# One block instead of two at the start of an encoder kernel: the modulation vectors and the input projection share one memory plan, and the first tile is modulated and split in halves

## The chip, the cores and the metric

The kernel runs on one core of one Trainium2 chip. A core has five engines that run side by side and meet through semaphores: TensorE (PE, matrix products into PSUM), VectorE (DVE), ScalarE (ACT), GpSimd (POOL) and SyncE (SP), which here does nothing but issue DMA transfers. The metric is the device time of one execution in microseconds (us).

## The reference

Two groups of rows (a prompt of 256 and a sample of 2048 rows, 1024 wide) go through one encoder layer with shared weights. What the change touches is its beginning:

```
mod = einsum('bd,de->be', silu(c), w_ada) + b_ada      # 2 x 6144
sh1, sc1, g1, sh2, sc2, g2 = split(mod, 6)
h = layer_norm(x) * (1 + sc1) + sh1
proj = einsum('bsd,de->bse', h, w_in)                  # 1024 -> 2048: q, k, v, u
lam = exp(sum(lq1 * lk1)) - exp(sum(lq2 * lk2)) + lambda_init
```

After that come rotary embedding, differential attention on q, k and v, a 2-D Fourier mix of u, an output projection, and a SwiGLU feed-forward part; they make up most of the time and are the same instructions in both kernels.

## The kernel before

The 2304 rows are 18 tiles of 128 rows (`NT`); tile `t` of the projection takes `x[ORDER[t]]`. The projection of a tile is 4 chunks of 512 columns by 8 blocks `k` of 128 inputs. For precision each product is made of three: both operands are split into a rounded high part and the remainder, and PE does hi times hi, hi times lo and lo times hi (`products`, L554 to L556). So a tile costs 96 products of 128x128 by 512 columns.

**The weights.** `w_in` comes in 32 pieces of 128x512 (256 KB; `w_in_piece(n)`, pieces 8c to 8c+7 belong to chunk c). Each piece passes three stations: SP loads it into one of four slots of the tile `ahead` (`w_raw`, `pair`), ACT copies it rounded into `w_hi`, DVE writes the remainder into `w_lo` (`split_w`, L240 in the first block, L690 in the second). A slot is free again when its remainder is written, so the load of piece n waits for `w_lo_done` of n-3, that is for the remainder of piece n-4. The high parts and remainders of all 32 pieces stay in memory for the other 17 tiles; only tile 0 has to wait for them.

**Two blocks.** A block is one program per engine between two barriers. `modulation` is the first. PE multiplies silu(c) by the two parts SH1 and SC1 of `w_ada`: eight steps `i` of 128 rows, each a pair of 512 KB loads into a ring of three slots `wa`, with 8 passes of 128x512 on PE (L213). DVE adds the bias (`add_bias`, L262), PE turns the rows into columns (L232), and DVE takes them (`take_cols`, L267). In between, the first two tiles of x are normalised on DVE (`norm`, L246 to L252), and tile 0 is transposed on PE (L222), modulated on DVE (L290, eight instructions, one for each k), copied rounded on ACT (L195) and its remainder taken on POOL (L205). SP issues all loads in one order, with the first 20 pieces of `w_in` between those of `w_ada`; 16 of them are also split. The block ends with some small DVE instructions for bias and lambda (L296 to L307).

At its end all engines meet at the block's barrier (L118), the semaphores of its scope are cleared, and they meet again (`Scope.release`, L74). Then `project` begins: PE transposes tile 1 (L549) and multiplies tile 0; DVE splits pieces 16 to 19, modulates tile 1 (L624), and splits pieces 20 to 31 with the normalisation of tile 2 after piece 27. Behind that DVE rotates q and k of tile 0 (`rotate`, L640 to L642). Chunk 0 of tile 1 may overwrite its PSUM bank when the rotation of tile 0's chunk 0 has read it (`turned_done`).

`project` itself ends with a barrier, the release of its own scope `proj`, and the release of the outer scope `w_in` that held what the two blocks shared; each release is a clearing of semaphores and a barrier.

Of the kernel before, what the change touches and what calls it, by code (L numbers as in the profile page):

```python
# [111 lines left out]
def modulation(nc, keep, first, x, rope, cT, w_ada, b_ada, lam_in, w_in, w_hi, w_lo):  # L112
# [4 lines left out]

    with ExitStack() as ctx:  # L118
        s = Scope(nc, ctx, "mod")
        RING, NCH = 3, 4  # L120
        wa = s.sb("wa", [P, RING, 2, D])
        c_in = s.sb("c_in", [P, KD, 2])
        c_silu = first["c_silu"]
        rows = s.sb("rows", [2, 2 * D])
        b_rows = s.sb("b_rows", [4 * KD, P])
        lam_v = s.sb("lam_v", [1, 4, QK])
        lam_p = s.sb("lam_p", [1, 2, QK])
# [2717 lines left out]
```

## Time and profile before

| what | value |
|---|---|
| median of 3 runs | 3055.91 us (3055.81 to 3057.52) |
| profiled execution | 3050.71 us, span of its instructions 3048.9 us |
| PE, DVE, ACT, POOL busy | 95%, 70%, 42%, 46% of the span |
| mean granted TensorE clock | 0.982 of full speed |

The span is the time from the first to the last instruction of one profiled execution; what lies around it is 1.8 us. "Idle before" in a row is the time that the engine stood still ahead of that instruction, with what ended the wait. The first block and the first tile of the second lie in the first 82 us of the span; the projection ends at about 504 us.

### The profile page before, as it was taken

Reading aid. Unit: us, or ns where it says so; the run is one execution under the profiler, and the core shown is the slowest. Engines: PE = TensorE matmul, PEld = TensorE weight load, DVE = VectorE, ACT = ScalarE, POOL = GpSimd, SP = SyncE. Lnnn points to the kernel's source line nnn. Section 1 sums busy time; section 2 is a strip of 40 time slices with the busy share of each in tenths; the row PEclk is TensorE's granted clock in tenths of the full one; section 3 lists DMA queues with packets and bytes.
Section 4 is the critical chain, followed back from the end, with each engine's and each line's share of the span. In section 5 each row is a group of like instructions: output and inputs, shape, how many; then the busy total and the mean of one; then the engine's idle time right before and its main releaser. Section 6 shows DMA issues by size and latency. Waiting matters only on the chain.

```text
span 3048.9 us, 39408 instructions
## 1 busy us (share of the span) xinstructions
PE 2902.0 (95%) x14244; PEld 2437.1 (80%) x14244; DVE 2139.3 (70%) x3093; ACT 1276.7 (42%) x2286; POOL 1409.1 (46%) x1110
## 2 busy tenths in 40 slices
PE   7999998899999998999689999999999999999996
PEld 3888886666666656888679999989999989999995
DVE  5666654988888865566566666677778666777767
ACT  2111112777777764456543233343333333333334
POOL 0233321011111125568745455475677566666655
PEclk9999999999999998999899999999999999999998
DMA  7333346221312105466431221242322224323322
GB/s 246 125 124 126 126 142 168 51 70 56 82 56 70 50 28 200 130 211 206 158 128 56 83 70 57 96 169 70 125 91 96 90 92 148 107 95 104 109 68 94
DMA packets 194061, 333.02 MB, mean 109 GB/s; under 512 B 15366, under 2 KB 102599, under 8 KB 193866
## 3 DMA queue, kind: packets, MB, share of 16 engines
q1 hardware_dynamic: 193868, 330.49, 33.5%
q8 instruction: 115, 1.88, 0.3%
q14 instruction: 78, 0.64, 0.1%
HBM read 250.72 MB, written 79.71 MB: 108 GB/s over the span
## 4 chain that ended last, share of the span: by engine, by line
PE 51%; POOL 3%; DVE 3%; issue 1%; DVEq 1%; POOLq 1%; ACT 1%; DMA 1%; SPq 0%; ACTq 0%
PE tail_bank L2306 9%; PE tail_bank L2308 9%; PE tail_bank L2307 9%; PE tail_bank L2330 5%; PE tail_bank L2331 5%; PE tail_bank L2332 5%; POOL tail_rounded L2042 1%; PE tail_bank L2245 1%; PE tail_bank L2243 1%; PE tail_bank L2244 1%; POOL tail_rounded L2050 1%; PE tail_bank L2192 0%; PE tail_bank L2184 0%; PE tail_bank L2185 0%; POOL tail_rounded L2055 0%
## 5 line engine op out<-in xcount | busy, mean ns | idle before, releaser
L2042 POOL TENSOR_TENSOR tail_rounded<-tail_plain,tail_rounded 128x512 fp32r<-128x512 f32 x462 | 649.2, 1426 | 490.8 <-ACT tail_rounded L1827 490.5
L2306 PE MATMUL tail_bank<-tail_rounded 128*128 128x384 f32 x1848 | 622.0, 337 | 35.4 <-ACT tail_plain L1847 10.4
L2307 PE MATMUL tail_bank<-tail_rounded 128*128 128x384 f32 x1848 | 620.4, 336 | 0.0
L2308 PE MATMUL tail_bank<-tail_rounded 128*128 128x384 f32 x1848 | 620.3, 336 | 0.0
L2466 DVE TENSOR_TENSOR tail_plain<-tail_plain,tail_bank 128x384 f32<-128x384 f32 x462 | 247.9, 549 | 283.8 <-PE tail_bank L2308 211.3
L1827 ACT ACTIVATE tail_rounded<-tail_plain 128x512 fp32r<-128x512 f32 x462 | 271.5, 621 | 377.3 <-DVE tail_plain L2444 184.3
L2306 PEld LDWEIGHTS tail_bank<-tail_rounded 128*128 128x128 f32 x1848 | 349.1, 189 | 39.8 <-issue 34.4
L2307 PEld LDWEIGHTS tail_bank<-tail_rounded 128*128 128x128 f32 x1848 | 349.2, 189 | 1.3
L2308 PEld LDWEIGHTS tail_bank<-tail_rounded 128*128 128x128 f32 x1848 | 349.0, 189 | 0.0
L1165 DVE TENSOR_REDUCE att_peak<-att_sc 128x1 f32<-128x1024 f32 x256 | 312.8, 1222 | 45.3 <-PE att_sc L978 38.5
L2330 PE MATMUL tail_bank<-tail_rounded 128*128 128x512 f32 x792 | 309.5, 391 | 16.1 <-issue 7.1
L1070 ACT ACTIVATE att_e<-att_sc,att_peak 128x1024 f32<-128x1024 f32 x256 | 285.4, 1115 | 80.4 <-DVE att_peak L1173 80.2
L2332 PE MATMUL tail_bank<-tail_rounded 128*128 128x512 f32 x792 | 309.5, 391 | 0.0
L2331 PE MATMUL tail_bank<-tail_rounded 128*128 128x512 f32 x792 | 309.4, 391 | 0.0
L2566 DVE TENSOR_TENSOR tail_plain<-tail_plain,tail_bank 128x512 f32<-128x512 f32 x348 | 230.8, 684 | 103.3 <-PE tail_bank L2332 99.0
L977 PE MATMUL att_sc<-held_w_hi 128*128 128x512 f32 x512 | 277.5, 542 | 20.9 <-ACT att_e L1070 13.4
L1015 PE MATMUL att_o<-att_w,att_v_s 128*128 128x512 f32 x512 | 260.3, 594 | 0.2 <-ACT att_o_sum L1081 0.2
L554 PE MATMUL proj_acc<-held_w_hi,w_in_h_hi 128*128 128x512 f32 x576 | 229.8, 399 | 0.0
L556 PE MATMUL proj_acc<-held_w_hi,w_in_h_lo 128*128 128x512 f32 x576 | 227.9, 396 | 0.0
L555 PE MATMUL proj_acc<-w_in_w_lo,w_in_h_hi 128*128 128x512 f32 x576 | 226.2, 393 | 0.0
L978 PE MATMUL att_sc<-held_w_hi 128*128 128x512 f32 x512 | 203.7, 398 | 0.0
L2330 PEld LDWEIGHTS tail_bank<-tail_rounded 128*128 128x128 f32 x792 | 149.1, 188 | 49.3 <-issue 8.0
(286 smaller groups left out, 5144.0 us busy)
## 6 DMA issues: line engine op xcount, KB each, us to landing
tail_plain<-in_w_gu SPq DMA_DIRECT2D x132, 512.0 KB, 4.8
keep_ahead<-in_w_dn SPq DMA_DIRECT2D x66, 512.0 KB, 6.6
proj_ada<-in_w_ada SPq DMA_DIRECT2D x16, 1024.0 KB, 5.9
held_w_hi<-scr_qs_d SPq DMA_DIRECT2D x128, 128.0 KB, 2.8
scr_h_d<-tail_plain SPq DMA_DIRECT2D x63, 256.0 KB, 4.5
tail_plain<-scr_h_d SPq DMA_DIRECT2D x45, 256.0 KB, 4.3
w_in_x_in<-in_x SPq DMA_DIRECT2D x18, 512.0 KB, 6.4
scr_att_d<-held_w_hi SPq DMA_DIRECT2D x36, 256.0 KB, 2.9
```

Of the source, the lines that this page charges most:

```text
L977: nc.tensor.matmul(dst, queries_at(w_hi, N // 2, 0, mp)[:, tokens], keys, start=True, stop=False)
L1015: ins = nc.tensor.matmul(o[:], v_s[:, m // (ST // 4) % 2, chunk, :], w[:, m % 2, chunk, :], start=(chunk == 0), stop=(chunk == ST - 1))
L1070: m = nc.scalar.activation(e[:, h * HALF:(h + 1) * HALF], sc[:, x % 3, :], ACT.Exp, bias=bias[:, 0:1], scale=SC, accum_out=sums[:, N % 2, ...
L1165: nc.vector.reduce_max(peak[:, N % 2, mp, h:h + 1], sc[:, x % 3, :], AX_X)
L1827: nc.scalar.activation(w_hi[:, j, :], operand(F, j), ACT.Copy).then_inc(whi_done, 1)
L2042: nc.gpsimd.tensor_tensor(w_lo[:, j, :], operand(F, j), w_hi[:, j, :].bitcast(F32), ALU.subtract).then_inc(wlo_done, 1)
L2306: nc.tensor.matmul(dst, w_hi[:, j, cols], h_hi[j][:, k, :], start=(k == 0), stop=False)
L2307: nc.tensor.matmul(dst, w_hi[:, j, cols], h_lo[j][:, k, :], start=False, stop=False)
L2308: m = nc.tensor.matmul(dst, w_lo[:, j, cols], h_hi[j][:, k, :], start=False, stop=(k == 3))
L2330: nc.tensor.matmul(dst, a_hi[:, i, c, tokens], dn_hi[:, i, cols], start=(i == 0), stop=False)
L2331: nc.tensor.matmul(dst, a_hi[:, i, c, tokens], dn_lo[:, i, cols], start=False, stop=False)
L2332: m = nc.tensor.matmul(dst, a_lo[:, i, c, tokens], dn_hi[:, i, cols], start=False, stop=(i == 1))
```

## The change

The two functions become one, `project`, with one block and one scope. Tiles that `modulation` had for itself now lie in tiles that the projection uses later: the ring `wa` in `ada`, `turned` and `u`, the bias rows in `work` (which also holds `part_sum`, `mid` and `v_out`), the lambda inputs in `h_raw`; the products of silu(c) go to `acc`, the columns, the bias and lambda to `qk_tp`. Gone are the barrier and the release between the blocks, and the release of the outer scope. The order on the engines changes in these places:

- the eight modulation instructions of tile 0 signal after the fourth (`h_half`); ACT and POOL make high part and remainder in two halves, and PE starts on the first four blocks k when the first half is there (`hlo_half`);
- PE transposes tile 1 after chunk 0 of tile 0 instead of ahead of it;
- ACT splits 10 pieces ahead of tile 0's high part (12 before) and pieces 10 to 17 behind it; DVE splits pieces 10 to 17 (`SPLIT_AHEAD`) ahead of tile 1's modulation, where it was 10 to 19;
- DVE splits pieces 0 to 2 between the normalisations of tiles 0 and 1;
- SP loads all 32 pieces in one stream, and tile 2 of x after piece 24, where it was after piece 19; the first load of `ada` has a wait for `ada_w_used` more;
- the small DVE instructions for bias and lambda stand behind piece 31, ahead of the first rotation.

```diff
-def modulation(nc, keep, first, x, rope, cT, w_ada, b_ada, lam_in, w_in, w_hi, w_lo):
...
+def project(nc, keep, x, cT, w_ada, b_ada, lam_in, mod_rows, w_in, w_hi, rope, qs_d, ks_d, v_d, up_d, fold_d, b0_d, mid_d, q_landed, k_first):
...
+        wa = [tile[:].rearrange(form).rearrange("p (h c) -> p h c", h=2) for tile, form in (
+            (ada, "p k c -> p (k c)"), (turned, "p a b c -> p (a b c)"), (u, "p k c -> p (k c)"))]
+        RING = len(wa)
+        rows = work[0:2].rearrange("r k c -> r (k c)")
...
+        SPLIT_AHEAD = 18
...
                 if u:
                     sp.wait_ge(half_done, u)
+                else:
+                    sp.wait_ge(ada_w_used, KD)
...
+            for n in range(pieces, PIECES):
+                piece(n)
+                if n == 3 * KD:
+                    load_x(2)
             load_ada(0)
...
-            for n in range(AHEAD, AHEAD + 4):
+            act.wait_ge(c_landed, 16)
+            nc.scalar.activation(c_silu[:], c_in[:], ACT.Silu).then_inc(silu_done, 1)
+            for n in range(10):
+                split_w(n)
+            act.wait_ge(h_half, 1)
+            nc.scalar.activation(h_hi[:, 0, 0:KD // 2, :], h_raw[:, 0:KD // 2, :], ACT.Copy).then_inc(hhi_half, 1)
+            act.wait_ge(h_done, 1)
+            nc.scalar.activation(h_hi[:, 0, KD // 2:, :], h_raw[:, KD // 2:, :], ACT.Copy).then_inc(hhi_done, 1)
+            for n in range(10, SPLIT_AHEAD):
                 split_w(n)
...
+            pool.wait_ge(hhi_half, 1)
+            nc.gpsimd.tensor_tensor(h_lo[:, 0, 0:KD // 2, :], h_raw[:, 0:KD // 2, :], h_hi[:, 0, 0:KD // 2, :].bitcast(F32),
+                                    ALU.subtract).then_inc(hlo_half, 1)
+            pool.wait_ge(hhi_done, 1)
+            nc.gpsimd.tensor_tensor(h_lo[:, 0, KD // 2:, :], h_raw[:, KD // 2:, :], h_hi[:, 0, KD // 2:, :].bitcast(F32),
+                                    ALU.subtract).then_inc(hlo_done, 1)
...
+            pe.wait_ge(hlo_half, 1)
             for t in range(NT):
-                if t + 1 < NT:
+                if 0 < t < NT - 1:
                     transposes(t + 1)
-                pe.wait_ge(hlo_done, t + 1)
+                if t:
+                    pe.wait_ge(hlo_done, t + 1)
...
                         if t == 0:
                             pe.wait_ge(w_lo_done, KD * c + k + 1)
+                            if c == 0 and k == KD // 2:
+                                pe.wait_ge(hlo_done, 1)
                         m = products(c, k, t % 2)
                     m.then_inc(chunk_done[c], 1)
+                    if c == 0 and t == 0:
+                        transposes(1)
...
                 if t == 0:
-                    for n in range(AHEAD + 4, PIECES):
+                    for n in range(SPLIT_AHEAD, PIECES):
                         split_w(n)
                         if n == PIECES - 5:
                             norm(2)
+                    dve.wait_ge(bias_turned, 1)
+                    nc.vector.tensor_copy(bias[:], bias_tp)
...
-        with ExitStack() as ctx_w:
-            weights = Scope(nc, ctx_w, "w_in")
```

**PE, from the last step of the modulation to the first products.** Before, from the sixteen small transposes of the modulation rows on:

```order
L232 MATMUL mod_cols<-keep_ident,mod_rows 128x2 x16
L118 UNCONDITIONAL_BRANCH
L540 UNCONDITIONAL_BRANCH
L549 MATMUL w_in_tp<-keep_ident,w_in_x_in 128x128 x8
L554 MATMUL proj_acc<-held_w_hi,w_in_h_hi 128x512
L555 MATMUL proj_acc<-w_in_w_lo,w_in_h_hi 128x512
L556 MATMUL proj_acc<-held_w_hi,w_in_h_lo 128x512
```

Now, where the 24 products of chunk 0 stand between the first and the last of these rows (L440 to L442 are the products, L435 the transposes of tile 1):

```order
L482 MATMUL proj_qk_tp<-keep_ident,proj_work 128x2 x16
L440 MATMUL proj_acc<-held_w_hi,proj_h_hi 128x512
L441 MATMUL proj_acc<-proj_w_lo,proj_h_hi 128x512
L442 MATMUL proj_acc<-held_w_hi,proj_h_lo 128x512
...
L435 MATMUL proj_tp<-keep_ident,proj_x_in 128x128 x8
L440 MATMUL proj_acc<-held_w_hi,proj_h_hi 128x512
```

The end of the block is gone from between them, and the transposes of tile 1 stand behind 24 products.

**DVE, from the normalisation of tile 0 to the splitting of the late pieces.** Before:

```order
L252 TENSOR_SCALAR w_in_x_in<-w_in_x_in,w_in_mv 128x1024
L246 BN_STATS w_in_stats<-w_in_x_in 128x6 x2
...
L240 TENSOR_TENSOR w_in_w_lo<-keep_ahead,held_w_hi 128x512 x10
L262 TENSOR_TENSOR mod_rows<-mod_acc,mod_rows 2x512 x4
L267 TENSOR_SCALAR keep_mod<-mod_cols 128x16 x2
L290 TENSOR_SCALAR w_in_h_raw<-w_in_tp,keep_mod 128x128 x8
L240 TENSOR_TENSOR w_in_w_lo<-keep_ahead,held_w_hi 128x512 x6
...
L690 TENSOR_TENSOR w_in_w_lo<-keep_ahead,held_w_hi 128x512 x4
L624 TENSOR_SCALAR w_in_h_raw<-w_in_tp,keep_mod 128x128 x8
L690 TENSOR_TENSOR w_in_w_lo<-keep_ahead,held_w_hi 128x512 x8
```

Now (L605 is `split_w`, L537 the modulation of a tile, L659 the first of the small instructions):

```order
L528 TENSOR_SCALAR proj_x_in<-proj_x_in,proj_mv 128x1024
L605 TENSOR_TENSOR proj_w_lo<-keep_ahead,held_w_hi 128x512 x3
L522 BN_STATS proj_stats<-proj_x_in 128x6 x2
...
L605 TENSOR_TENSOR proj_w_lo<-keep_ahead,held_w_hi 128x512 x7
L615 TENSOR_TENSOR proj_work<-proj_acc,proj_work 2x512 x4
...
L605 TENSOR_TENSOR proj_w_lo<-keep_ahead,held_w_hi 128x512 x8
L537 TENSOR_SCALAR proj_h_raw<-proj_tp,keep_mod 128x128 x8
L605 TENSOR_TENSOR proj_w_lo<-keep_ahead,held_w_hi 128x512 x10
...
L605 TENSOR_TENSOR proj_w_lo<-keep_ahead,held_w_hi 128x512 x4
L659 COPY proj_bias<-proj_qk_tp 128x32
```

Between the modulation of tile 1 and the last piece there were 8 + 4 = 12 pieces, and there are now 10 + 4 = 14.

**SP, the second half of the stream of pieces.** Before:

```order
L160 DMA mod_wa<-in_w_ada 128x1024 x2
L151 DMA keep_ahead<-in_w_in 128x512 x11
L118 UNCONDITIONAL_BRANCH
L360 UNCONDITIONAL_BRANCH
L372 DMA w_in_x_in<-in_x 128x1024
L411 DMA keep_ahead<-in_w_in 128x512 x12
L368 DMA proj_ada<-in_w_ada 128x4x512
```

Now:

```order
L258 DMA proj_turned<-in_w_ada 128x1024 x2
L249 DMA keep_ahead<-in_w_in 128x512 x16
L210 DMA proj_x_in<-in_x 128x1024
L249 DMA keep_ahead<-in_w_in 128x512 x7
L206 DMA proj_ada<-in_w_ada 128x4x512
```

The load of tile 2 of x (512 KB) moved from ahead of piece 20 to behind piece 24.

## Rows read from the trace of the kernel before

**Rows 1.** The page, busy time of each engine over the whole span:

```profile
PE 2902.0 (95%) x14244; PEld 2437.1 (80%) x14244; DVE 2139.3 (70%) x3093; ACT 1276.7 (42%) x2286; POOL 1409.1 (46%) x1110
```

**Rows 2.** All waits of PE from 80 to 503 us: total, times, longest:

```profile
PE w_in_tp L573 <- DVE w_in_h_raw L624: 3.2, 3, 1.9
```

**Rows 3.** Timeline of PE: start, us, instructions, [idle before <-releaser]:

```profile
25.11 3.60 PE L213 MATMUL mod_acc<-mod_wa,w_in_c_silu 128*2 128x512 f32 x8 [1.86 <-DMA mod_wa<-in_w_ada]
...
30.72 3.60 PE L213 MATMUL mod_acc<-mod_wa,w_in_c_silu 128*2 128x512 f32 x8 [0.99 <-DMA mod_wa<-in_w_ada]
...
35.02 3.59 PE L213 MATMUL mod_acc<-mod_wa,w_in_c_silu 128*2 128x512 f32 x8 [0.30 <-DMA mod_wa<-in_w_ada]
38.93 3.59 PE L213 MATMUL mod_acc<-mod_wa,w_in_c_silu 128*2 128x512 f32 x8 [0.32 <-DMA mod_wa<-in_w_ada]
43.38 1.15 PE L232 MATMUL mod_cols<-keep_ident,mod_rows 2*128 2x2 f32 x16 [0.85 <-DVE mod_rows L262]
55.35 1.94 PE L549 MATMUL w_in_tp<-keep_ident,w_in_x_in 128*128 128x128 f32 x8 [10.83 <-PEq L74]
56.95 0.78 PE L554 MATMUL proj_acc<-held_w_hi,w_in_h_hi 128*128 128x512 f32 x1
...
81.27 0.47 PE L554 MATMUL proj_acc<-held_w_hi,w_in_h_hi 128*128 128x512 f32 x1
```

**Rows 4.** Timeline of DVE in the same stretch:

```profile
44.90 2.64 DVE L290 TENSOR_SCALAR w_in_h_raw<-w_in_tp,keep_mod 128x128 f32<-128x128 f32 x8
...
53.32 0.17 DVE L296 COPY w_in_bias<-mod_cols 128x32 f32<-128x32 f32 x1
...
58.52 2.64 DVE L624 TENSOR_SCALAR w_in_h_raw<-w_in_tp,keep_mod 128x128 f32<-128x128 f32 x8
62.81 4.29 DVE L690 TENSOR_TENSOR w_in_w_lo<-keep_ahead,held_w_hi 128x512 fp32r<-128x512 f32 x4 [1.65 <-ACT held_w_hi L464]
...
72.28 1.28 DVE L609 BATCH_NORM_STATS2 w_in_stats<-w_in_x_in 128x6 f32<-128x512 f32 x2
...
77.61 0.69 DVE L690 TENSOR_TENSOR w_in_w_lo<-keep_ahead,held_w_hi 128x512 fp32r<-128x512 f32 x1 [0.25 <-ACT held_w_hi L464]
78.23 0.68 DVE L640 TENSOR_TENSOR proj_turned<-proj_acc,w_in_rot 128x512 f32<-128x512 f32 x1
...
79.49 0.68 DVE L640 TENSOR_TENSOR proj_turned<-proj_acc,w_in_rot 128x512 f32<-128x512 f32 x1
```

**Rows 5.** Timelines of ACT and POOL, tile 0's high part and remainder:

```profile
47.57 1.06 ACT L195 ACTIVATE w_in_h_hi<-w_in_h_raw 128x1024 fp32r<-128x1024 f32 x1 [6.02 <-DVE w_in_h_raw L290]
48.70 2.34 POOL L205 TENSOR_TENSOR w_in_h_lo<-w_in_h_raw,w_in_h_hi 128x1024 fp32r<-128x1024 f32 x1 [26.76 <-ACT w_in_h_hi L195]
```

**Rows 6.** Timeline of SP: issue of pieces 3 and 4, pair 5 of `w_ada`, pieces 24 on:

```profile
18.65 5.12 SPq L151 DMA_DIRECT2D keep_ahead<-in_w_in  x2
23.82 0.98 SPq L160 DMA_DIRECT2D mod_wa<-in_w_ada  x2
...
65.33 7.39 SPq L411 DMA_DIRECT2D keep_ahead<-in_w_in  x8
```

**Rows 7.** Timeline of ACT: it waits for piece 24:

```profile
68.56 0.63 ACT L464 ACTIVATE held_w_hi<-keep_ahead 128x512 fp32r<-128x512 f32 x1 [4.22 <-DMA keep_ahead<-in_w_in]
```

**Rows 8.** The tile `ahead`, to 82 us: remainders of the second block (min/median/max ns), time to landing:

```profile
L690 DVE TENSOR_TENSOR w_in_w_lo<-keep_ahead,held_w_hi x16: 677/692/2487, 55.8 to 77.6; 128x512 fp32r<-128x512 f32 x16
...
DMA to landing us min/median/max: 2.8/4.3/7.8
```

**Rows 9.** Stretches: length, busy of PE, PEld, DVE, ACT, POOL, clock, DMA, GB/s:

```profile
46.00:46.50 0.50, 0.00 (x0) 0.00 (x0) 0.50 (x3) 0.00 (x0) 0.00 (x0) 0.93 0.00 0
60.00:60.50 0.50, 0.50 (x3) 0.37 (x2) 0.50 (x3) 0.00 (x0) 0.00 (x0) 0.92 0.82 287
527.00:528.00 1.00, 1.00 (x5) 0.62 (x4) 1.00 (x2) 0.61 (x2) 0.00 (x0) 0.86 1.07 199
```

**Rows 10.** The releases' line at the end of the projection: first and last start:

```profile
L74 POOLq EVENT_SEMAPHORE  x4: 17/17/17, 511.0 to 511.6; - x4
```

More of the change, by code:

```diff
@@ L109 @@
 LATER = (SH2 * D, SC2 * D, G1 * D, G2 * D)
-def modulation(nc, keep, first, x, rope, cT, w_ada, b_ada, lam_in, w_in, w_hi, w_lo):
+def project(nc, keep, x, cT, w_ada, b_ada, lam_in, mod_rows, w_in, w_hi, rope, qs_d, ks_d, v_d, up_d, fold_d, b0_d, mid_d, q_landed, k_first):
     with ExitStack() as ctx:
[L119 to L127, printed above, removed]
+        s = Scope(nc, ctx, "proj")
+        NCH = 4
+        w_lo = s.sb("w_lo", [P, KD, WIDTH], F32R)
+        x_in = s.sb("x_in", [P, 2, D])
+        h_raw = s.sb("h_raw", [P, KD, P])
+        h_hi, h_lo = s.sb("h_hi", [P, 2, KD, P], F32R), s.sb("h_lo", [P, 2, KD, P], F32R)
+        rot = s.sb("rot", [P, 2, 2, QK])
+        stats, mv = s.sb("stats", [P, 2, 2, 6]), s.sb("mv", [P, 2, 4])
+        pair = keep["ahead"]
+        turned = s.sb("turned", [P, 2, 2, 512])
+        u = s.sb("u", [P, 4, 512])
+        ada = s.sb("ada", [P, KD // 2, 512])
+        work = s.sb("work", [P, 4, 512])
+        part_sum, mid, v_out = work[:, 0:2, :], work[:, 2, :], work[:, 3, :]
+        qk_hi = s.sb("qk_hi", [P, 2, HEADS, P], F32R)
+        qk_lo = s.sb("qk_lo", [P, 2, HEADS, P], F32R)
+        gate_cols = s.sb("gate_cols", [P, 2, 2, KD])
+        gate_rows = s.sb("gate_rows", [4 * KD, P])
+        bias = s.sb("bias", [P, 4 * KD])
+        c_in, c_silu = s.sb("c_in", [P, KD, 2]), s.sb("c_silu", [P, KD, 2])
         lam_s = s.sb("lam_s", [1, 8])
@@ L310, in project @@
[L310 to L329 removed]
+        tp = s.ps("tp", [P, KD, P])
@@ L471, in _ @@
                 if t == 0:
-                    for n in range(AHEAD + 4, PIECES):
+                    for n in range(SPLIT_AHEAD, PIECES):
                         split_w(n)
@@ L625, in modulate @@
                                                   keep["mod"][:, k, g:g + 1], ALU.mult, ALU.add)
+                    if t == 0 and k == KD // 2 - 1:
+                        ins.then_inc(h_half, 1)
                 ins.then_inc(h_done, 1)
@@ L702, in _ @@
                 if t == 0:
-                    for n in range(AHEAD + 4, PIECES):
+                    for n in range(SPLIT_AHEAD, PIECES):
                         split_w(n)
@@ L2743, in layer @@
         }
-        ahead = s.sb("ahead", [P, 4, 512])
+        keep["ahead"] = ahead = s.sb("ahead", [P, 4, 512])
         ctx_h = ctx.enter_context(ExitStack())
```

323 lines of the change are left out of this document (119 added, 204 removed).

## The prediction

> **What bounds the kernel now.** I read the page first: PE is busy for 95% of the span, every other engine for 70% or less [rows 1]. So a change of 80 us at the start can only pay by what it lets PE do earlier, and only if PE is then never again waiting for something that did not move. The waits of PE come next. From 80 us to the end of the projection at about 504 us PE waits 3.2 us in all, in three places of 18 tiles [rows 2]: from tile 1 on the projection is PE after PE, and the attention and the rest have the same instructions as before. The number to follow is therefore one: when does chunk 0 of tile 1 start? It starts at 81.27 us [rows 3]. Whatever it gains or loses reaches the end of the kernel, with what the end of the block changes.
>
> The timeline of PE shows what stands ahead of it. The modulation's four last pairs of `w_ada` start at 25.11, 30.72, 35.02 and 38.93 us, each after a wait for DMA, 8 passes in 3.6 us each; the last small transposes start at 43.38; then PE stands still for 10.83 us until 55.35, and the first product comes at 56.95 [rows 3]. In the gap lie the modulation of tile 0 on DVE (44.90 to 47.54), its high part on ACT (47.57 to 48.63), its remainder on POOL (48.70 to 51.04), and then only pieces, the small instructions from 53.32 on, and the barrier [rows 4, 5]. From the first product to tile 1 it is 81.27 - 56.95 = 24.3 us without a wait. The time spent there is PE's own. But the pieces are close behind: the remainder of piece 31 is finished at 77.61 + 0.69 = 78.30 us [rows 4], only some 1.5 us before PE reads it. What is to be seen: PE can start tile 0 ten microseconds earlier, but can it also end ten microseconds earlier? The stream of pieces decides that.
>
> **Part 1, the modulation.** SP issues pieces 3 and 4 from 18.65 us on and is held for 5.12 us, since piece 4 waits for the remainder of piece 1, which DVE, busy with and waiting for the normalisation of tile 1, has only by 23.3; so pair 5 goes out at 23.82 [rows 6]. The change takes piece 0's split ahead of that normalisation. SP's wait is for the count of remainders, one for piece 4, and is then met at about 18.3. Pair 5 can go out when PE has used pair 2, at about 20. Between the starts of pairs 6 and 7 lie 3.91 us, and in them the queue moved two pieces and a pair (1.57 MB); between the starts of pairs 4 and 5 it moved as much in 5.61 us [rows 3]. The difference, 1.7 us, is the emptiness that the early issue fills. PE's own work then binds: pair 4 at 25.11, its passes and tile 0's transposes to 29.7, and three more pairs of 3.5 us, with 0.5 us of small work, to 40.8; before it was 38.93 + 3.5 = 42.4. I take **1.6 us earlier** for everything that follows; the bounds are 0 and 1.7.
>
> **Part 2, the start of tile 0.** Modulation starts at 44.90 - 1.6 = 43.3. Half of it is 1.32 us; the half high part is an ACT instruction of the size of a piece, 0.63 us [rows 7]; half of POOL's 2.34 us [rows 5] is 1.2; with a tenth for each hand-over PE starts at 46.8, against 56.95 before. The second half is ready at 48.1, ahead of PE's need.
> PE starts slowly: the granted clock fell at about 46.4, two microseconds after PE's last work, and rose at about 60.0, 4.7 us after it began again [rows 9]. With the gap of about 3.8 us that is left I expect the same: to 51.3 at 1.2 GHz, a product each 0.43 us, then one each 0.229 us. Chunk 0 ends at 54.4, the transposes of tile 1 at 55.2.
>
> **Part 3, the pieces.** Here each step waits for the one before. ACT no longer splits pieces 10 and 11 early, so DVE has them at 48.6 and 49.2; a remainder that meets POOL's instruction waits for its end. (That is how I read the longest remainder, 2487 ns where the median is 692 [rows 8]: it starts at 62.81 [rows 4] beside POOL's remainder of tile 1.) The Trainium skill, "SBUF — State Buffer", section "SBUF: two separate sides", says the same: GpSimd and a DVE instruction with two SBUF inputs take one pair of ports by an exclusive lock, held for the whole instruction. By that rule the modulation of tile 0, which reads PSUM, would not be held by POOL's first half.
> Pieces 14 to 17 follow their slots and are done at 53.2 to 55.1. DVE then modulates tile 1 (2.64 us, [rows 4]) from 55.3 to 58.0. ACT and POOL follow to 61.5, and POOL holds the remainder of piece 18 until 62.05; 19 to 21 follow by 63.9.
> Now the ring of four sets the pace. Piece 24 was issued at 65.33 and ACT had it at 68.56, 3.2 us later [rows 6, 7]; the median to landing is 4.3 us [rows 8]. With 0.65 us on ACT and 0.69 on DVE a slot turns round in 4.6 to 6.4 us, and a burst of four lands about 0.9 us apart. Piece 22 (slot of 18) is done at 66.7, 23 to 25 by 69.3, where the load of x for tile 2 lies in the queue ahead of 25; 26 at 71.5, 27 at 72.3. Then come the normalisation of tile 2 and pieces 28 to 31, which before took from 72.28 to 78.30, 6.0 us with 0.25 of waiting [rows 4]; without the wait it is 5.8, and piece 31 is done at about **78.0 us**, against 78.30. The same stretch before gives the same: from the end of tile 1's modulation (58.52 + 2.64) to piece 31 it was 17.1 us for 12 pieces [rows 4]; from 58.0 with 14 pieces, the two more at 1 to 1.5 us each, it is 77 to 78.
> PE, ready early, waits for pieces from 22 on and ends tile 0 at 78.7.
>
> **Part 4, the small instructions.** They took from 53.32 to about 54.4 [rows 4]: 1.05 us. Before they lay under a wait of PE; now they stand between piece 31 and the rotation that PE waits for. The rotation of one chunk takes 79.49 - 78.23 = 1.26 us [rows 4]. So chunk 0 of tile 1 starts at 78.0 + 1.05 + 1.3 = **80.4 us**, against 81.27: 0.9 us gained. With PE's own end and the 0.8 us of transposes it would be 79.5; the rotation binds.
>
> **Part 5, the end of the block.** Two releases follow each other there, 0.5 to 0.6 us apart [rows 10]. One goes: **0.5 us gained**. Everything else costs nothing that I can find: the wait for `ada_w_used` was met 30 us before, and the order within tiles 1 to 17 is the same.
>
> **Sum.** 0.9 + 0.5 = 1.4 us. Against the profiled execution, 3050.7 us, that gives 3049.3; the median of the runs lies 5.2 us above that execution, so I forecast 3055.9 - 1.4 = **3054.5 us**. Ten microseconds of earlier start become one and a half. The bounds of part 3: with every slot at 3.2 us to landing piece 31 is done at 77.7, with every slot at 4.3 at 79.0, which makes 0.4 to 1.7 us of gain, and 0 instead of 1.6 in part 1 takes up to 1.6 off. Its own range is 3053.9 to 3056.5.
>
> **The rivals.**
> *The clock falls while PE waits for pieces.* From 65 to 77 PE would be busy about half of the time, with one gap of 3 us at the normalisation. In the attention, with waits between groups of products, the granted clock was 0.86 from 527 to 528 us [rows 9]: there it fell again. If it falls here, 4.7 us at 1.2 GHz lose 4.7 x (1 - 0.229/0.43) = 2.2 us at the start of tile 1: 0.8 us slower than before, 3056.7. I give it 0.2.
> *The loads keep pace.* If pieces land as fast as DVE can split them, only DVE binds: from 62.05 nine remainders of 0.63 (pieces 19 to 27) and the 5.8 us behind them give 73.5, the rotation is done at 75.8, and the gain is 5.5 + 0.5 = about 6 us: 3050. For it speaks that the queue is emptier than in the first 40 us; against it, ACT's wait of 4.22 us for piece 24 with nothing but pieces on the way [rows 7]. 0.12 for a gain of 3 to 6 us; 0.05 for more, which needs the clock to stay up through the first gap too.
> *The pieces fall behind.* A landing took up to 7.8 us [rows 8], where pairs of 1 MB were in the queue. If both turns of the ring from piece 22 on meet that, each is 3.5 us longer than at 4.3, piece 31 is done at about 86, and the kernel is 6 us slower, 3062. It decides only from an average landing above 7.5 us; in that stretch there are only 512 KB of x and, behind the last piece, 1 MB for `ada`. 0.05.
> *The change does nothing that counts*, a gain within 0.3 us: that is the lower edge of the forecast and has its number.
>
> **How the numbers follow.** The forecast has 0.58. About 0.2% (6 us) is what a measurement of this kernel tells from no change. Faster by more needs the second rival's far end, 0.06; slower by more the third, 0.05; the rest, 0.89, is within. The range holds the forecast, the clock and most of the second rival: 3050 to 3058.
>
> **What the trace after would show.** PE's pairs of `w_ada` without the 1 us wait at pair 5; the first product at about 47 us and not near 57; then waits of PE for DVE's remainders from about piece 22 on, and piece 31's remainder at 78 us; the small instructions right ahead of the first rotation, chunk 0 of tile 1 at 80.4; a single release at the end of the projection. I am wrong if the remainder of piece 31 is done before 75 or after 81, if the clock is at half speed when tile 1 starts, or if tiles 2 to 17 show waits that were not there.

## The result, and the profile after

The changed kernel takes 3061.38 us (median of 15 runs, 3054.97 to 3068.91), the kernel before 3052.15 us (15 runs, 3049.54 to 3057.52). The ratio is 1.0030, its 95% interval 1.0023 to 1.0038: slower by 0.3%, some 9 us, where 1.4 us less was forecast.

The profiled execution took 3061.82 us, its span is 3060.0 us (before 3048.9). Its start went much as forecast in this execution. Timeline of PE, to set beside [rows 3]:

```profile
23.96 3.59 PE L467 MATMUL proj_acc<-proj_turned,proj_c_silu 128*2 128x512 f32 x8 [1.60 <-DMA proj_turned<-in_w_ada]
...
28.51 3.60 PE L467 MATMUL proj_acc<-proj_u,proj_c_silu 128*2 128x512 f32 x8
...
36.49 3.60 PE L467 MATMUL proj_acc<-proj_turned,proj_c_silu 128*2 128x512 f32 x8 [0.33 <-DMA proj_turned<-in_w_ada]
40.88 1.15 PE L482 MATMUL proj_qk_tp<-keep_ident,proj_work 2*128 2x2 f32 x16 [0.80 <-DVE proj_work L615]
45.83 0.79 PE L440 MATMUL proj_acc<-held_w_hi,proj_h_hi 128*128 128x512 f32 x1 [3.79 <-POOL proj_h_lo L406]
...
65.97 0.50 PE L440 MATMUL proj_acc<-held_w_hi,proj_h_hi 128*128 128x512 f32 x1 [1.59 <-DVE proj_w_lo L605]
...
75.80 0.50 PE L440 MATMUL proj_acc<-held_w_hi,proj_h_hi 128*128 128x512 f32 x1 [1.15 <-DVE proj_w_lo L605]
...
79.96 0.47 PE L440 MATMUL proj_acc<-held_w_hi,proj_h_hi 128*128 128x512 f32 x1 [0.26 <-DVE proj_turned L557]
```

The last row is chunk 0 of tile 1, 1.3 us earlier than before. Ahead of it PE waits for pieces, and DVE's timeline, to set beside [rows 4], has piece 31 done at 77.55, the six small instructions from 77.47 on, and then the rotation:

```profile
58.84 4.29 DVE L605 TENSOR_TENSOR proj_w_lo<-keep_ahead,held_w_hi 128x512 fp32r<-128x512 f32 x4 [1.65 <-ACT held_w_hi L334]
...
75.06 2.49 DVE L605 TENSOR_TENSOR proj_w_lo<-keep_ahead,held_w_hi 128x512 fp32r<-128x512 f32 x4
77.47 0.19 DVE L659 COPY proj_bias<-proj_qk_tp 128x32 f32<-128x32 f32 x1
...
78.46 0.69 DVE L555 TENSOR_TENSOR proj_turned<-proj_acc,proj_rot 128x512 f32<-128x512 f32 x1
```

So in this execution the changed kernel is ahead at 82 us. But the first product of the attention (L977 before, L940 after) shows it 7.7 us behind. Timelines of PE, of before and then of after:

```profile
511.88 0.77 PE L977 MATMUL att_sc<-held_w_hi 128*128 128x512 f32 x1 [7.56 <-PEq L74]
```

```profile
519.58 0.76 PE L940 MATMUL att_sc<-held_w_hi 128*128 128x512 f32 x1 [8.43 <-PEq L74]
```

Nine microseconds went between these two places, eight of them in tiles 1 to 17, where the order of every engine is that of before. (The rest, from there to the end, took 2537.0 us before and 2540.4 after. In the executions told of below it lies between 2533 and 2546 without relation to the edits, so nothing is read from it.) The waits of PE from 80 to 511 us, which answer to [rows 2], say where:

```profile
PE proj_tp L459 <- DVE proj_h_raw L537: 7.9, 3, 3.0
PE proj_acc L440 <- DVE proj_turned L557: 0.3, 1, 0.3
```

It is the same line as before, the small products that add the partitions of `part_sum`, with 7.9 us in place of 3.2. They wait for `h_done`, tile t+1's modulation. The three places are tiles 6, 10 and 14. Timeline of PE before:

```profile
217.62 1.92 PE L573 MATMUL w_in_tp<-keep_ones,proj_part_sum 128*128 128x1 f32 x16 [1.91 <-DVE w_in_h_raw L624]
...
319.15 1.92 PE L573 MATMUL w_in_tp<-keep_ones,proj_part_sum 128*128 128x1 f32 x16 [1.11 <-DVE w_in_h_raw L624]
```

and after, with the transposes that stand at the start and the end of tile 6:

```profile
200.62 1.09 PE L435 MATMUL proj_tp<-keep_ident,proj_x_in 128*128 128x128 f32 x8
...
216.51 2.59 PE L459 MATMUL proj_tp<-keep_ones,proj_work 128*128 128x1 f32 x16 [3.00 <-DVE proj_h_raw L537]
232.49 1.03 PE L435 MATMUL proj_tp<-keep_ident,proj_x_in 128*128 128x128 f32 x8
...
320.00 3.55 PE L459 MATMUL proj_tp<-keep_ones,proj_work 128*128 128x1 f32 x16 [2.18 <-DVE proj_h_raw L537]
...
424.02 1.94 PE L459 MATMUL proj_tp<-keep_ones,proj_work 128*128 128x1 f32 x16 [2.70 <-DVE proj_h_raw L537]
```

After the change the granted clock falls behind each of the three; before, it fell behind the first alone. Stretches of before (columns: length, busy of PE, clock, DMA, GB/s), then the same of after:

```profile
220.00:230.00 10.00, 10.00 (x38) 0.83 0.53 149
...
320.00:330.00 10.00, 10.00 (x50) 1.00 0.54 151
...
420.00:430.00 10.00, 10.00 (x45) 1.00 0.58 179
```

```profile
220.00:230.00 10.00, 10.00 (x37) 0.78 0.52 143
...
320.00:330.00 10.00, 10.00 (x38) 0.66 0.41 113
...
420.00:430.00 10.00, 7.30 (x34) 0.83 0.04 10
```

Taken from one tile's transposes to the next, tiles 6, 10 and 14 last 31.87, 31.00 and 29.94 us after, and 29.29, 26.89 and 25.97 before: 10.7 us more. The fourteen others of tiles 1 to 17 are 0.18 us shorter each (23.56 for 23.75, 25.37 for 25.54), 2.5 us less; the start gives 1.3 in this execution; the gap ahead of the attention costs 0.9. That is 7.8 us, and 7.7 were found.

Why is DVE late there? Behind its modulation stands a loop whose pace PE does not set: beside the projection the later parts of `w_ada` are multiplied on DVE, 1 MB at a time, in the tile `ada`. Such a load lands, DVE adds its rows and modulates and rotates, SP, which waits for the rotation, issues the rope load, four stores of `qs_d` and `ks_d`, in every fourth tile four of `fold_d`, the store of `v_d`, and only then the next `ada`. Tile 4's pass of SP, before:

```profile
174.76 0.59 SPq L396 DMA_DIRECT2D scr_ks_d<-proj_qk_hi  x1
175.39 0.56 SPq L396 DMA_DIRECT2D scr_ks_d<-proj_qk_lo  x1
176.08 2.09 SPq L403 DMA_DIRECT2D scr_fold_d<-proj_u  x4
...
178.79 0.33 SPq L429 DMA_DIRECT2D scr_v_d<-proj_v_out  x1
179.17 0.46 SPq L368 DMA_DIRECT2D proj_ada<-in_w_ada  x1
```

and after:

```profile
172.89 0.56 SPq L234 DMA_DIRECT2D scr_ks_d<-proj_qk_hi  x1
173.50 0.79 SPq L234 DMA_DIRECT2D scr_ks_d<-proj_qk_lo  x1
174.41 3.02 SPq L241 DMA_DIRECT2D scr_fold_d<-proj_u  x4
...
178.04 0.54 SPq L299 DMA_DIRECT2D scr_v_d<-proj_work  x1
178.62 0.45 SPq L206 DMA_DIRECT2D proj_ada<-in_w_ada  x1
```

The same DMAs of the same size take longer to issue: from the `ks_d` store out of `qk_hi` to `ada` it was 4.41 us and is 5.73. The loop takes 23.5 us from DVE's modulation at 190.21 to the one at 213.73, and PE's tile 5 takes 23.58, so what it loses in a fold tile it still lacks two tiles later, at the first products of the sums. In tile 6 DVE is ready for `ada` at 200.56 and has it at 207.92:

```profile
207.92 5.89 DVE L586 SCALAR_TENSOR_TENSOR proj_work<-proj_ada,proj_c_silu,proj_work 128x512 f32<-128x512 f32 x8 [7.36 <-DMA proj_ada<-in_w_ada]
213.73 2.64 DVE L537 TENSOR_SCALAR proj_h_raw<-proj_tp,keep_mod 128x128 f32<-128x128 f32 x8
```

PE had come to the sums at 213.51 (216.51 less the wait of 3.00).

### The profile page after: what moved, and what is told of

It is laid out like the page before. It is cut to its first block, busy times and chain, and to the rows that moved or that the text cites. A ratio compares the mean times of both kernels' runs of the same rounds, so it can differ in the third digit from the quotient of the medians.

```text
span 3060.0 us, 39374 instructions
## 1 busy us (share of the span) xinstructions
PE 2910.4 (95%) x14244; PEld 2444.4 (80%) x14244; DVE 2147.2 (70%) x3093; ACT 1276.7 (42%) x2287; POOL 1408.2 (46%) x1111
## 4 chain that ended last, share of the span: by engine, by line
PE 50%; POOL 4%; DVE 4%; issue 1%; DVEq 1%; DMA 1%; ACT 1%; POOLq 1%; SPq 0%; ACTq 0%
PE tail_bank L2269 9%; PE tail_bank L2271 9%; PE tail_bank L2270 9%; PE tail_bank L2293 5%; PE tail_bank L2295 5%; PE tail_bank L2294 5%; POOL tail_rounded L2005 2%; PE tail_bank L2206 1%; PE tail_bank L2207 1%; PE tail_bank L2208 1%; POOL tail_rounded L2018 1%; POOL tail_rounded L2013 1%; PE tail_bank L2147 0%; PE tail_bank L2155 0%; PE tail_bank L2148 0%
## 5 line engine op out<-in xcount | busy, mean ns | idle before, releaser
L940 PE MATMUL att_sc<-held_w_hi 128*128 128x512 f32 x512 | 277.8, 543 | 21.0 <-ACT att_e L1033 12.6
L440 PE MATMUL proj_acc<-held_w_hi,proj_h_hi 128*128 128x512 f32 x576 | 233.4, 405 | 7.6 <-POOL proj_h_lo L406 3.8
L441 PE MATMUL proj_acc<-proj_w_lo,proj_h_hi 128*128 128x512 f32 x576 | 228.4, 397 | 0.0
L442 PE MATMUL proj_acc<-held_w_hi,proj_h_lo 128*128 128x512 f32 x576 | 228.2, 396 | 0.0
```

The lines of the kernel that those rows point to most:

```text
L940: nc.tensor.matmul(dst, queries_at(w_hi, N // 2, 0, mp)[:, tokens], keys, start=True, stop=False)
```

## The experiments

Three theories. **T1:** PE reaches the sums earlier than before, the loop does not, and the longer waits bring the clock down. **T2:** the new addresses slow the stores and with them the loop. **T3:** the merged block itself costs. Each time is a median, each ratio is against the kernel before on the same chip, with its 95% interval (the medians come from four sets of runs, not all on one chip, so kernels are compared by the ratios); "ks" is the issue of the `ks_d` store from `qk_lo` (median of the projection), "fold" that of tile 4's four fold stores.

| kernel | us | ratio | ks, us | fold, us | waits at 6, 10, 14 |
|---|---|---|---|---|---|
| before | 3052.15 | | 0.57 | 2.09 | 1.91, 1.11, 0.18 |
| changed | 3061.38 | 1.0030 (1.0023 to 1.0038) | 0.82 | 3.02 | 3.00, 2.18, 2.70 |
| p1_oldplan | 3055.16 | 1.0004 (0.9995 to 1.0012) | 0.57 | 2.08 | 1.11, 0.55, 0.49 |
| p1_sums_late | 3051.24 | 0.9983 (0.9972 to 0.9993) | 0.82 | 3.01 | none |
| p1_ada_early | 3048.77 | 0.9978 (0.9967 to 0.9989) | 0.83 | 3.00 | none |
| p1_before_ada_early | 3050.91 | 0.9985 (0.9977 to 0.9994) | 0.57 | 2.18 | none |
| p2_pad320 | 3052.00 | 0.9999 (0.9986 to 1.0011) | 0.57 | 2.06 | 1.40, 0.97, 0.46 |
| p2_old_shifted | 3061.33 | 1.0032 (1.0020 to 1.0044) | 0.81 | 3.00 | 2.54, 1.64, 2.24 |
| p2_h_shifted | 3057.61 | 1.0022 (1.0010 to 1.0034) | 0.80 | 3.00 | 2.36, 1.48, 1.84 |
| p2_pad320_early | 3045.58 | 0.9971 (0.9961 to 0.9982) | 0.57 | 2.17 | none |
| p3_before_shifted | 3062.18 | 1.0026 (1.0017 to 1.0035) | 0.84 | 3.01 | 2.91, 2.04, 2.24 |
| p3_all512_early | 3047.26 | 0.9976 (0.9967 to 0.9985) | 0.57 | 2.17 | none |

**The old addresses in the new block.**

```
+        c_silu, bias = s.sb("c_silu", [P, KD, 2]), s.sb("bias", [P, 4 * KD])
         h_raw = s.sb("h_raw", [P, KD, P])
...
+        ada = s.sb("ada", [P, KD // 2, 512])
+        part_sum = s.sb("part_sum", [P, 2, 512])
+        gate_cols = s.sb("gate_cols", [P, 2, 2, KD])
+        gate_rows = s.sb("gate_rows", [4 * KD, P])
         u = s.sb("u", [P, 4, 512])
...
+        v_out = s.sb("v_out", [P, 512])
```

> The changed kernel with the buffers of the projection at the addresses that they had before the change (c_silu and bias behind x_in; ada, part_sum, gate_cols, gate_rows, u, mid, qk_hi, qk_lo, v_out in the old order; the row of biases in a tile of its own behind them). Order of instructions as in the changed kernel. Theory T2 (the new addresses slow the stores of qk and fold, and so the loop of VectorE, SyncE's queue and the transfer of ada): the issue of the ks store from qk_lo falls from 0.82 us to 0.57, four fold stores from 3.0 to 2.1 us, undisturbed tiles are 23.75 and 25.54 us again, PE's waits ahead of the sums at tiles 6, 10 and 14 fall from 3.0, 2.2 and 2.7 us to about 2, 1 and 0, and the time is 3049 to 3053 us (the kernel before, less the 1.3 us won by 82 us). Theory T1 (PE's earlier arrival alone, with the clock that falls behind each wait): nothing changes, 3058 to 3064 us. Theory T3 (a cost of the merged block itself): likewise unchanged.

Measured: store issues and tiles (23.74 and 25.55 us) as before the change, two of the three waits shorter, no difference to the kernel before that can be told; at 3055.16 us it is slower than the 3049 to 3053 expected. T3 falls: the block is as merged as in the changed kernel. T1 had expected no change here, but as the tiles are slower again PE's arrival moved as well; what settles T1 are p2_pad320 and p3_before_shifted below.

**The sums one chunk later.**

```
-                    if c == 1 and closes_sum(t):
+                    if c == 2 and closes_sum(t):
```

> The changed kernel with the 8 small products of the sums behind chunk 2 in place of chunk 1. Both T1 and T2 put the whole loss on the three waits there and on the clock that falls behind each: tiles 6, 10 and 14 go from 31.9, 31.0 and 29.9 us towards 25.4, the clock is full from 200 to 450 us, at most 17 us less, 3044 to 3050 us; the lateness of VectorE and SyncE's queue is then no longer recovered by PE's waits and can come up at another wait, at most 10 us of it again, so 3044 to 3055. If the waits are not the cause (T3), 3058 to 3064.

Measured: no wait at the sums. The stores are still slow, and the lateness comes up elsewhere: PE waits 3.8 us in three places ahead of the transposes, for the normalisation:

```profile
PE proj_tp L435 <- DVE proj_x_in L528: 3.8, 3, 1.7
```

So part of the gain is given back, and the time is inside what was expected.

**`ada` ahead of the stores**, in the changed kernel and in that of before.

```
-                if 1 < t <= HALVES:
-                    load_ada(t - 1)
                 if 0 < t < NT - 2:
                     load_x(t + 2)
+                if 0 < t < HALVES:
+                    load_ada(t)
```

> The changed kernel with the load of the next half of ada issued in front of the rope load and the stores of its loop pass, so as soon as the buffer is free, in place of behind them. It takes the stores out of the loop: VectorE no longer waits 7 to 9 us in each tile, PE waits nowhere ahead of the sums, tiles 6, 10, 14 take 25.4 us, clock 1.0 from 90 to 511 us: 17 us less, 3044 to 3047 us, by T1 and by T2 alike. T3: 3058 to 3064.

> The kernel before with the same earlier load of ada. Its waits at tiles 6, 10 and 14 (1.91, 1.11 and 0.18 us, tiles of 29.3, 26.9 and 26.0 us where 25.5 is undisturbed) go: 5.6 us less, 3045 to 3048 us. With the loop gone on both sides the changed kernel should be the faster one by what it wins by 82 us (1.3 us) and by its shorter tiles (0.19 us in each of 17, 3.2 us), so by 2 to 5 us, if T2's address effect acts on the loop alone. If the changed kernel stays slower even so, something outside the loop costs.

Measured: DVE's timeline of p1_ada_early in tile 6 has the modulation within 4 us of the tile's start, and what it waits for is PE, not `ada`:

```profile
204.26 2.65 DVE L537 TENSOR_SCALAR proj_h_raw<-proj_tp,keep_mod 128x128 f32<-128x128 f32 x8 [1.43 <-PE proj_tp L435]
```

Tiles 6, 10 and 14 take 25.37 us, and the attention's first product is at 505.62 us, 14 us earlier than in the changed kernel. In the kernel before it is 508.00, 3.9 us earlier. Both medians lie above the expected ranges, but in the same set of runs the kernel before took 3054.10 us. By the ratios p1_ada_early is 0.52% below the changed kernel, 16 us (the intervals leave 10 to 22) where 14 to 17 stood, and p1_before_ada_early 0.15% below the kernel before, 4.6 us (2 to 7) where 5.6 stood: no shortfall is shown. With the loop gone the changed kernel is 2.1 us below the other, in one set of runs. The intervals of the two ratios overlap, so it is no loss, and a gain isn't shown.

**Only where the rows begin.** The addresses of the built program show one thing: before, `u`, `mid`, `qk_hi`, `qk_lo` and `v_out` began at a multiple of 512 bytes; after, they begin 192 bytes behind one.

```
+        pad = s.sb("pad", [P, 80])
         turned = s.sb("turned", [P, 2, 2, 512])
```

> The changed kernel with 320 bytes left empty ahead of turned, so that turned, u, ada, work, qk_hi and qk_lo begin at a multiple of 512 bytes (before the change u, mid, qk_hi, qk_lo and v_out did; in the changed kernel they stand 192 bytes behind one); order of the buffers and everything else as in the changed kernel. Theory T2a (the start of the rows that are stored, against 512 bytes, sets what a store costs): the ks store from qk_lo issues in 0.57 us and four fold stores in 2.1, as before the change, and PE's waits ahead of the sums fall from 3.0, 2.2 and 2.7 us to about 2.3, 1.5 and 0.5 (before's 1.9, 1.1 and 0.2 plus 0.36 for two tiles shorter by 0.17 and 0.19 us), 3048 to 3056 us. Theory T2b (the order or place of the buffers, not the start against 512): 0.82 and 3.0 us, 3058 to 3064 us. The tiles stay at 23.56 us if the shorter tiles hang on where h_hi and h_lo begin, which don't move here.

Measured: 320 empty bytes give back the whole loss, though the tiles stay at 23.57 us and PE comes to the sums of tile 6 at 215.48, no later than before the change (215.71). So T1 alone falls. Tile 4's pass of SP:

```profile
174.94 0.59 SPq L235 DMA_DIRECT2D scr_ks_d<-proj_qk_hi  x1
175.57 0.57 SPq L235 DMA_DIRECT2D scr_ks_d<-proj_qk_lo  x1
176.26 2.06 SPq L242 DMA_DIRECT2D scr_fold_d<-proj_u  x4
```

**The reverse, in both kernels:** 192 empty bytes ahead of `u`, in p1_oldplan and in the kernel before, which has nothing of the change.

```
+        pad = s.sb("pad", [P, 48])
         u = s.sb("u", [P, 4, 512])
```

> The kernel of p1_oldplan (old order and addresses) with 192 bytes left empty ahead of u, so that u, mid, qk_hi, qk_lo and v_out begin 192 bytes behind a multiple of 512, as they do in the changed kernel, all else at its old place. T2a: stores as slow as in the changed kernel (0.82 and 3.0 us), tiles of 23.75 and 25.54 us, the waits at tiles 6, 10 and 14 about 2.6, 1.8 and 2.3 us, and 3057 to 3063 us. T2b: 0.57 and 2.1 us, and the 3055 us of p1_oldplan.

> The kernel before, untouched but for 192 bytes left empty ahead of u, so that u, mid, qk_hi, qk_lo and v_out begin 192 bytes behind a multiple of 512 as in the changed kernel. If the place of these five buffers is the cause (T2a), the kernel before gets the whole loss without any of the change: ks store from qk_lo 0.82 us, four fold stores 3.0 us, waits ahead of the sums at tiles 6, 10 and 14 of about 2.6, 1.9 and 2.1 us where 1.9, 1.1 and 0.2 stood, and 3057 to 3063 us. If the merged block is needed for the loss, 3052 to 3055 us.

Measured: both get the whole loss, 1.0032 and 1.0026. The tiles of the kernel before with 192 empty bytes begin within 0.03 us of those of the kernel before, up to tile 6. Tile 4's pass of SP, to set beside that of before above:

```profile
174.76 0.55 SPq L397 DMA_DIRECT2D scr_ks_d<-proj_qk_hi  x1
175.35 0.84 SPq L397 DMA_DIRECT2D scr_ks_d<-proj_qk_lo  x1
176.31 3.01 SPq L404 DMA_DIRECT2D scr_fold_d<-proj_u  x4
...
179.84 0.55 SPq L430 DMA_DIRECT2D scr_v_d<-proj_v_out  x1
180.44 0.45 SPq L369 DMA_DIRECT2D proj_ada<-in_w_ada  x1
```

The first store goes out at the same hundredth, 174.76; `ada` goes out at 180.44 for 179.17. All waits of PE from 80 to 503 us in it:

```profile
PE w_in_tp L574 <- DVE w_in_h_raw L625: 7.2, 3, 2.9
```

The first of them, in its timeline:

```profile
218.63 1.92 PE L574 MATMUL w_in_tp<-keep_ones,proj_part_sum 128*128 128x1 f32 x16 [2.91 <-DVE w_in_h_raw L625]
```

PE arrives at 215.72, in the kernel before at 215.71 (217.62 less 1.91): the wait is longer by 1.0 us without any earlier arrival. Nor does the engines' own work on the moved buffers take longer: in both kernels ACT writes a chunk into `u` in 0.60 us, and DVE writes the first part of `u` in tile 4 in 0.69 and `qk_lo` in 1.21.

**h_hi and h_lo shifted, the stores left slow.** 192 bytes are left empty ahead of `h_raw`, and 320 ahead of `turned`.

> The changed kernel with h_raw, h_hi, h_lo, rot, stats and mv 192 bytes further on, where they stood before the change against 512 bytes (256 behind a multiple), and 320 bytes left empty behind them, so that turned to qk_lo stay 192 behind one. It tells whether the shorter tiles (23.56 for 23.75 us) come from where h_hi and h_lo begin (then 23.75 again), and what a slower PE does while the loop of VectorE and the queue stays slow: T1 (PE's early arrival makes the waits) has the waits at tiles 6, 10 and 14 shorter by 0.4 us and the clock falling less often, so no more than 3062 us although 16 tiles are 0.19 us longer; if arrival doesn't matter, 3 us more than the changed kernel, 3064 us.

Measured: the tiles are 23.75 and 25.54 us again, so where `h_hi` and `h_lo` begin sets the 0.18 us; the waits are shorter by 0.6 to 0.9 us. The intervals of this kernel and of the changed one overlap: whether PE's later arrival gains as much as its slower products cost isn't told apart. T1 holds as a part (arrival sizes the wait), not as the cause. p4_at64 below fits: its stores are as slow, its tiles 24.15 us long, and its waits 0.73, 0.53 and 0.88 us.

**The two remedies together, and everything at a multiple of 512.** The second has 448 empty bytes ahead of the buffer of the pieces and 384 in place of 320 ahead of `turned`.

> p2_pad320 with the earlier load of ada of p1_ada_early. The loop is gone, so the stores' cost is hidden: the same as p1_ada_early, 3045 to 3050 us; if the misplaced stores cost elsewhere too (k stores ahead of the attention, other transfers in the same DMA engines), 1 to 3 us less than p1_ada_early.

> p2_pad320_early with 448 bytes left empty ahead of the buffer of the pieces too, so that it, w_hi, w_lo, x_in, h_raw, h_hi and h_lo begin at a multiple of 512 bytes (64 behind one in all other runs), turned to qk_lo as there. If only stores out of SBUF gain by it, 3045 us again and tiles of 23.58 us; if PE's reads or the landing of pieces and of q and k (same buffer as w_hi) gain too, tiles shorter than 23.5 us or a shorter attention, 3038 to 3044 us; if h at 64 was the good place, tiles of 23.75 us and 3048 us.

Measured: 3045.58 us is the lowest median, 0.3% below the kernel before and, by the ratios, 0.6% below the changed one. Against p1_ada_early the ratio is lower by 0.0007, 2 us, and the intervals overlap; in the traces it is 0.9 us ahead at the attention's first product (504.71 for 505.62). So a gain of the padding besides that of the early load isn't shown. Placing the targets of the loads as well gave nothing: `ada` lands in 5.4 us either way, tiles 23.54 us.

**The halves alone.** In the changed kernel `h_hi` and `h_lo` of tile 0 are made whole by one instruction each on ACT and on POOL.

> The changed kernel with the first tile's h_hi and h_lo made whole again (one instruction on ScalarE, one on GpSimd) and nothing else changed. It sizes the halves alone: the first product 2.3 to 3 us later (48.2 to 48.8 us for 45.8), and since PE waits 3.4 us in total for pieces of w_lo between 62 and 80 us, chunk 0 of tile 1 no more than 0.5 us later (80.0 to 80.5 us for 79.96) if those pieces are what binds there; 2.5 us later if they are not. The loss behind 82 us stays.

Measured (one run, 3058.65 us): the first product comes 7.72 us behind the start of the small transposes, where with the halves it is 4.94 to 4.96 us in all 13 executions, so the halves bring it 2.8 us forward. Chunk 0 of tile 1 is at 82.79, 2.8 later than in the changed kernel's profile, but that one is early by chance: in the 12 other executions with the halves it starts between 81.39 and 84.03. Whether anything of the halves' gain reaches tile 1 is not shown, neither the 0.5 us at most that I expected nor more.

**How far off a multiple.** One run each, with 64 empty bytes ahead of `turned` in the first; in the others 64, 128 and 256 ahead of `h_raw` and 64, 64 and 32 ahead of `turned`.

> The changed kernel with 64 bytes left empty ahead of turned: turned to qk_lo begin 256 bytes behind a multiple of 512. If what counts is 512, stores cost as in the changed kernel (0.82 us, four of fold 3.0 us); if 256 or 64 are enough, as before the change (0.57 and 2.1 us). The time of one run says little here; the issues do.

> The changed kernel with turned to qk_lo 64 bytes behind a multiple of 256 (0 behind one they were fast, 192 behind one slow) and h_hi and h_lo 128 behind a multiple of 512. Theory S (a transfer is cut at multiples of 256 bytes of SBUF, and a cut piece costs by the 256 bytes that it begins in): a row of 512 bytes costs 18 beats for 16, an eighth more, and the ks store from qk_lo would issue in 0.57 x 1.125 = 0.64 us, four fold stores in 2.35. Theory A (any start that is no multiple of 256 costs the same): 0.82 and 3.0 us. By the way: tiles of 23.56 us if h is well placed at 128 behind a multiple of 512, 23.75 if not.

> The same with turned to qk_lo 128 bytes behind a multiple of 256, h_hi and h_lo 192 behind a multiple of 512. S: 20 beats for 16, a quarter more, 0.71 us for the ks store and 2.6 for four fold stores. A: 0.82 and 3.0 us.

> The same with turned to qk_lo 224 bytes behind a multiple of 256, h_hi and h_lo 320 behind a multiple of 512. S: 23 beats for 16 where 192 behind has 22, so 0.86 us for the ks store and 3.15 for four fold stores. A: 0.82 and 3.0 us.

Measured: the tile `ks_d`, the stores from `qk_lo` (issue ns min/median/max), of p3_pad64 (256 behind a multiple of 512), p4_at64, p4_at128 and p4_at224:

```profile
L235 SPq DMA_DIRECT2D scr_ks_d<-proj_qk_lo x18: 559/574/2325, 98.9 to 502.9; - x18
```

```profile
L236 SPq DMA_DIRECT2D scr_ks_d<-proj_qk_lo x17: 614/834/1690, 98.8 to 500.3; - x17
```

```profile
L236 SPq DMA_DIRECT2D scr_ks_d<-proj_qk_lo x16: 695/834/879, 99.3 to 490.6; - x16
```

```profile
L236 SPq DMA_DIRECT2D scr_ks_d<-proj_qk_lo x17: 699/842/1638, 99.7 to 499.9; - x17
```

A multiple of 256 is as good as one of 512, and every start off it costs the same: theory A, not S. The times of these single runs, 3051.82 and 3060.11, 3063.51 and 3063.68 us, go the same way. p4_at64 and p4_at128 have another cost besides, tiles of 24.15 and 24.11 us, from `h` at 128 and 192 behind a multiple of 512.

## Why the prediction was wrong

**Part 1** gave 1.6 us; the small transposes came at 40.88 for 43.38, 2.5 us earlier. In 13 other executions of the new block they came between 39.80 and 43.11, the middle one at 41.64, 1.7 us earlier than 43.38: the term was right, and the landings of the pairs scatter it by more than its size. **Part 2** gave 46.8 us for the first product; it was 45.83, and 53.48 for the transposes of tile 1 (forecast 54.4).

**Part 3** gave 78.0 us for piece 31; 77.55 was measured, with PE's waits for pieces from about 66 us on. **Part 4**, 1.05 us of small instructions: 0.99. Chunk 0 of tile 1: 80.4 forecast, 79.96 measured, so 1.3 us gained for 0.9. But this execution was a lucky one. In the 12 other executions of the new block with the halves, piece 31 is done between 77.74 and 81.63, the middle at 79.9, and in the six of them whose small transposes start at 41.4 to 41.9, as part 1 has it, at 78.9 to 80.5. So part 3 was about 2 us too short; what took longer there stays open. Chunk 0 of tile 1 starts between 81.39 and 84.03 in the 12, the middle at 82.6 (some of their edits lengthen tile 0, by 0.6 us at most), and in three executions of the old block at 81.27, 81.28 and 82.93. A gain of the start is not shown over these, and the ratio of p1_oldplan, 1.0004, says the same.

**The rival of the falling clock**, given 0.2, is part of why. In the profiled execution of the changed kernel the granted clock was 0.50 from about 67 to 74 us, while PE waited for pieces, and 1.00 again ahead of tile 1. In each of the 12 others it fell as well between 66 and 84 us, and in seven of them it was below 1.00 from 78 to 80 us, right ahead of tile 1. In p1_oldplan it fell a second time, right there (columns: length, busy of PE, clock, DMA, GB/s):

```profile
76.00:78.00 2.00, 0.89 (x4) 1.00 0.50 142
78.00:80.00 2.00, 2.00 (x7) 0.61 0.82 310
```

**Part 5** gave 0.5 us for the release. Where the stores are well placed, PE's gap ahead of the attention is 7.33, 7.42 and 7.50 us (p1_oldplan, p2_pad320, p3_pad64) for 7.56, so 0.1 to 0.2 us; with the early load it is 7.56 and 6.84. In the changed kernel it is 8.43, and in the nine others whose stores are off a multiple of 256 it is 7.66 to 8.59.

**The sum.** The range that the prediction works out for itself, 3053.9 to 3056.5 us, does not follow from its bounds: gains of 0.4 to 1.7 us, less up to 1.6, make 3054.2 to 3057.1. The forecast doesn't hang on it.

The step that failed is the sentence behind the release in part 5: "Everything else costs nothing that I can find", with the order in tiles 1 to 17 being the same as its reason. The order was the same. The addresses were not. I went through what the change moves in time and did not go through what it moves in memory, though that is half of its name. The diff shows that the buffers are allocated anew, and the sizes in it give every address: `c_silu`, `bias`, `gate_cols` and `gate_rows`, 64 + 128 + 128 + 512 = 832 bytes, stood ahead of `u` and went behind it. That is 320 more than 512, so `u` and what follows moved from a multiple of 512 to 320 bytes short of one, which is 192 behind the next lower. What the runs show in the place of nothing is 0.3%, some 9 us: p2_pad320 takes it away and p3_before_shifted makes it. The second half of the miss is [rows 2]: I read three waits of 3.2 us as "PE after PE" and did not ask what stood behind them. A loop as long as PE's tile stood there, without slack, so that 1.3 us more in it each fold tile became 4.7 us of waits and, with the clock, 10.7 us in three tiles. The last sentence of the prediction names the sign that came true: waits in tiles 2 to 17 that were not there, here 4.7 us more in the three places.

Shown are the chain from where rows begin to the time (p2_pad320, p2_old_shifted, p3_before_shifted, both ways and in both kernels), and the loop's part (p1_ada_early, p1_sums_late). The Trainium skill, "DMA: Bandwidth & Descriptors", section "How a descriptor splits into AXI transactions", says that a transfer is cut at multiples of 256 bytes and that bytes ahead of its start in the first cut are fetched for nothing. By that rule a row of 512 bytes is cut into 3 in place of 2 when it begins off such a multiple. The traces agree on the boundary: 256 behind a multiple of 512 is fast, 64, 128, 192 and 224 behind one of 256 are slow. On the amount they don't. An estimate by that section's rule gives such a row 18, 20, 22 and 23 beats (units of the transfer) for 16, so the cost should grow with the offset; the issue took 0.80 to 0.84 us for 0.57 at every one, and the time to landing was 3.6 us (3.5 in p2_h_shifted) for 2.9 to 3.0 at every one. That the number of cuts sets it, 3 for 2, would fit 0.83 / 0.57 = 1.46, but the fold stores, whose rows of 2048 bytes that rule cuts into 9 for 8, grow as much, 3.02 / 2.09 = 1.44. So what sets the amount stays open.

## What to carry to other kernels

A new memory plan is a change of its own: list where each buffer that is stored from begins, before and after. Here 320 empty bytes, which bring them to a multiple of 256, were worth 9 us of 3050. And a small wait of the busiest engine that comes back at a fixed period can be the sign of a second loop without slack. Here issuing the load ahead of the stores took it out of that loop, and what was slow in the loop was hidden. And one profiled execution is not the kernel: the start looked 1.3 us faster in it, and over 12 others nothing of that was left.

## What was unexpected of the hardware

- The store of 256 KB from `qk_lo` to `ks_d` issues in 0.57 us or in 0.80 to 0.84, by the first byte's place in SBUF alone. The three stores ahead of it issue in about 0.43, 0.51 and 0.55 to 0.59 in every kernel: only those queued behind show it in their issue. In the time to landing the earlier ones show it too: 2.9 us for 2.6 in the second. Loads into SBUF show nothing of it: `ada` lands in 5.4 us at 192 behind a multiple of 512 and at 0.
- PE's products take 2 to 6 ns more or less by where `h_hi` and `h_lo` begin: tiles of 23.54, 23.56 and 23.56 us at 0, 64 and 320 behind a multiple of 512, 23.75 at 256, 24.15 at 128 and 24.11 at 192. Why stays open.
- A short wait can cost more than itself. The twelve traces with waits at the sums have 36 of them. Each of the 24 from 1.26 us up made its tile 1.8 to 3.5 us longer than the wait alone, as the clock fell. Of the twelve from 0.18 to 1.11 us, eight cost 0.2 to 0.3 us besides and four, of 0.53, 0.55, 0.73 and 0.88 us, cost 1.8. So the length of the wait alone doesn't decide it.
